# One level of Strassen's product for the mLSTM values and output gates of a hybrid decoder layer

## The reference, cut to what matters

```python
hin = _rms_norm(x, norm_g[0])
z = hin @ w_in                      # (512 x 1024) @ (1024 x 2964)
(mq, mk, mv, lq, lk, lv, lo, li, lf,
 nq, kc, vc, ksl, vsl, kwn, vwn, ng) = jnp.split(z, split_points, axis=-1)
...
qk = silu(causal_conv(concat([lq, lk])))     # 4 groups of 128 features
y_ml = mlstm(lq, lk, lv, li + gate_b[0], lf + gate_b[1])
y = concat([head_norm(y_moba), head_norm(y_ml) * sigmoid(lo), head_norm(y_nsa)])
```

## Time and profile before

| | before |
|---|---|
| median of 3 runs | 603.61 us |
| the profiled execution | 603.88 us |
| its span | 602.1 us |
| PE busy | 590.5 us (98%) |
| DVE, ACT, POOL busy | 390.1, 300.0, 257.0 us |

### The profile page before, as it was taken

One profiled execution on the slowest core, in us unless ns is written; L12 is line 12 of the kernel. 1 busy time (PEld: TensorE's weight loads), 2 busy tenths in 40 slices (PEclk: granted clock), 3 DMA queues, 4 the chain that ended last, 5 costly groups with the idle time before them and its releaser, 6 DMA issues.

```text
span 602.1 us, 8286 instructions
## 1 busy us (share of the span) xinstructions
PE 590.5 (98%) x3095; PEld 484.5 (80%) x3095; DVE 390.1 (65%) x666; ACT 300.0 (50%) x529; POOL 257.0 (43%) x138
## 2 busy tenths in 40 slices
PE   8999999999999999999999999999999999999995
PEld 5898888877866678899878888888888888888884
DVE  6414605266978774983999777585595685771656
ACT  6713414654589934555645545444355265354322
POOL 7763323573094610043357443631723626611611
PEclk9999999999999999999999999999999999999998
DMA  8743282466023710028034340621603404104002
GB/s 326 288 144 137 72 208 71 87 161 208 1 45 104 264 63 0 1 72 280 1 143 137 136 144 1 209 71 67 202 12 139 141 0 153 57 1 175 1 35 106
DMA packets 36580, 67.18 MB, mean 112 GB/s; under 512 B 2876, under 2 KB 23612, under 8 KB 35516
## 3 DMA queue, kind: packets, MB, share of 16 engines
q1 hardware_dynamic: 36236, 66.25, 34.0%
q10 hardware_dynamic: 304, 0.39, 0.3%
HBM read 62.18 MB, written 2.10 MB: 107 GB/s over the span
## 4 chain that ended last, share of the span: by engine, by line
PE 89%; ACT 4%; DVE 3%; issue 2%; DMA 1%; SPq 0%; POOLq 0%; POOL 0%; ACTq 0%; DVEq 0%
PE ps L1814 19%; PE ps L1816 19%; PE ps L1815 19%; PE ps L2288 7%; PE ps L2290 7%; PE ps L2289 7%; PE ps L2140 2%; PE ps L2155 2%; PE ps L2051 1%; PE ps L2052 1%; ACT probs L949 1%; DMA x_land<-in_x_turned 1%; ACT W L890 1%; PE ps L1979 1%; PE ps L2216 1%
## 5 line engine op out<-in xcount | busy, mean ns | idle before, releaser
L1814 PE MATMUL ps<-xT_h,ring_h 128*128 128x512 f32 (+1 forms) x384 | 144.3, 376 | 0.3 <-DVE q_far L1361 0.3
L1816 PE MATMUL ps<-xT_h,ring_l 128*128 128x512 f32 (+1 forms) x384 | 143.2, 373 | 0.0
L1815 PE MATMUL ps<-xT_l,ring_h 128*128 128x512 f32 (+1 forms) x384 | 143.1, 373 | 0.0
L773 POOL TENSOR_TENSOR ring_l<-raw_d,ring_h 128x1024 fp32r<-128x1024 f32 x25 | 67.3, 2699 | 129.8 <-ACT ring_h L1044 129.8
L773 POOL TENSOR_TENSOR ring_l<-raw,ring_h 128x1024 fp32r<-128x1024 f32 x31 | 76.7, 2499 | 77.5 <-DVE xres L1630 38.1
L692 POOL TENSOR_TENSOR ring_l<-raw,ring_h 128x512 fp32r<-128x512 f32 (+2 forms) x26 | 64.2, 2489 | 74.1 <-ACT ring_h L796 74.1
L1724 DVE TENSOR_TENSOR y<-ps,y 128x512 f32<-128x512 f32 x90 | 61.2, 689 | 50.9 <-PE ps L2290 50.6
L1814 PEld LDWEIGHTS ps<-xT_h,ring_h 128*128 128x128 f32 x384 | 72.4, 188 | 14.0 <-issue 1.3
L1816 PEld LDWEIGHTS ps<-xT_h,ring_l 128*128 128x128 f32 x384 | 72.3, 188 | 12.9
L1815 PEld LDWEIGHTS ps<-xT_l,ring_h 128*128 128x128 f32 x384 | 72.4, 189 | 12.5
L2288 PE MATMUL ps<-ring_h,a_h 128*128 128x512 f32 x196 | 76.7, 391 | 0.1
(11 more groups left out here) (276 smaller groups left out, 994.7 us busy)
## 6 DMA issues: line engine op xcount, KB each, us to landing
raw<-in_w_mlp SPq DMA_DIRECT2D x16, 1024.0 KB, 5.6
raw_d<-in_w_mlp SPq DMA_DIRECT2D x16, 1024.0 KB, 6.1
raw<-in_w_groups SPq DMA_DIRECT2D x8, 1024.0 KB, 4.8
xres<-in_x SPq DMA_DIRECT2D x8, 512.0 KB, 6.3
raw<-in_nsa_cmp_w SPq DMA_DIRECT2D x8, 512.0 KB, 6.6
raw<-in_w_groups SPq DMA_DIRECT2D x8, 256.0 KB, 5.5
raw<-in_w_out SPq DMA_DIRECT2D x2, 1024.0 KB, 6.2
raw<-in_w_out SPq DMA_DIRECT2D x4, 512.0 KB, 4.8
```

The costliest lines, as they stand in the source:

```text
L773: nc.gpsimd.tensor_tensor(slot(ring_l, n), slot_source(n), slot(ring_h, n).bitcast(F32), ALU.subtract).then_inc(lo_done, 1)
L1814: nc.tensor.matmul(o, sh, mh, start=start, stop=False)
L1815: nc.tensor.matmul(o, sh, ml, start=False, stop=False)
L1816: return nc.tensor.matmul(o, sl, mh, start=False, stop=stop)
```

## The change

`lv` and `lo` are now one product (512 x 1024 by 1024 x 1024) in Strassen's form (Winograd's variant): seven products of 256 x 512 by 512 x 512, each 24 matmuls of 512 columns. They need four sums of blocks of x (`s_h`, `s_l`), four sums of weight blocks (`t_sum`, made on DVE from landed chunks), and DVE adds of the results. Group B is now the first group, in slabs of 404 columns; then `lq`, `lk`, then the seven products, three of loaded weights and x sums first. Seven chunks (11, 22, T2, 21, T3, T4, T1) have their low halves cut into four POOL instructions of 512 columns.

```diff
-READER = "vvvv" "vvvv" "vvvv" "aaaa" "v" ...
+READER = "vvvv" "vvvv" "vvvvvvvv" "v" ...
+C_11, C_22, C_T2, C_21, C_T3, C_T4, C_T1 = range(C_S, C_S + 7)
+CHUNK_ORDER = [C_LK, C_T1, C_11, C_22, C_21, C_KVS, C_NQ, C_CMP + 2, ...]
 # SP
+                if c == C_22:
+                    sp.wait_ge(xl_ready, NC + 2)
...
 # POOL
+                step = SEQ if C_S <= c < C_KVS or c >= C_WO else n
+            low_half(C_LQ)
+            def sum_low(n, order):
+                pool.wait_ge(xh_ready, NC + order)
+                nc.gpsimd.tensor_tensor(s_l[n][:], s_raw[n][:], s_h[n][:].bitcast(F32), ALU.subtract).then_inc(xl_ready, 1)
+            sum_low(2, 2)
+            sum_low(0, 3)
+            low_half(C_LK)
+            low_half(C_11)
+            sum_low(3, 4)
+            low_half(C_22)
...
-            for c in range(2, C_CMP):
+            for c in range(C_T2, C_MK + 1):
                 low_half(c)
 # ACT
-            high_half(2)
-            for t in range(NT):
-                x_root(t)
-            for c in (3, 4, 5, 6):
-                high_half(c)
+            high_half(C_LQ)
+            x_root(0)
+            x_root(1)
+            act.wait_ge(x_scaled, NC + 3)
+            for n in (1, 2, 0):
+                sum_high(n)
+            x_root(2)
+            x_root(3)
+            high_half(C_LK)
+            sum_high(3)
+            high_half(C_11)
...
+                if n == 2:
+                    high_half(C_T2)
+            for t in range(2):
+                act.wait_ge(part_used, 2)
+                nc.scalar.activation(first_p[t][:], ps[:, t, :], ACT.Copy).then_inc(first_copied, 1)
+            high_half(C_21)
...
+            high_half(C_T3)
+            high_half(C_T4)
+            high_half(C_T1)
+            high_half(C_KVS)
+            high_half(C_NQ)
 # DVE, beside and behind the eight slabs of x
+                if k < 4:
+                    nc.vector.scalar_tensor_tensor(s_raw[2][:, k, :], x_all[:, k, TH:SEQ], gain_cols[:, k:k + 1], ps[:, 4 + k, 0:TH], ALU.mult, ALU.subtract)
+            for k in range(4):
+                last = nc.vector.scalar_tensor_tensor(s_raw[0][:, k, :], ..., ps[:, 4 + k, TH:SEQ], ALU.mult, ALU.add)
+            nc.vector.tensor_tensor(late, late, s_raw[2][:], ALU.add).then_inc(x_scaled, 1)
+            for k in range(4, NC):
+                last = nc.vector.scalar_tensor_tensor(s_raw[3][:, k - 4, :], ..., ps[:, k, TH:SEQ], ALU.mult, ALU.subtract)
+            nc.vector.tensor_tensor(s_l[1][:], late, s_h[1][:].bitcast(F32), ALU.subtract).then_inc(x_scaled, 1)
...
+            def weight_sum(c):
+                if c == C_T3:
+                    made = nc.vector.tensor_tensor(t_sum[0][:], raw[2][:], raw[3][:], ALU.subtract)
+                elif c == C_T2:
+                    made = nc.vector.tensor_tensor(t_sum[1][:], raw[0][:], t_sum[0][:], ALU.subtract)
+                elif c == C_T4:
+                    dve.wait_ge(lo_done, split_no(C_21) + 1)
+                    made = nc.vector.tensor_tensor(raw[1][:], raw[1][:], t_sum[1][:], ALU.subtract)
+                else:
+                    made = nc.vector.tensor_tensor(raw[2][:], raw[2][:], raw[0][:], ALU.subtract)
...
 # PE
-            pe.wait_ge(xl_ready, 2 * NT)
-            token_group(J_B, C_B, BN)
...
             feature_group(J_CONV, C_LQ)
             feature_group(J_CONV + 2, C_LK)
-            token_group(J_LO, C_LO, 512)
+            values_and_gates()
+                product(C_11, *low, 0, 0, True, part_used, ...)
+                product(C_22, s_h[3], s_l[3], 0, 4, True, part_used, ...)
+                product(C_T2, s_h[1], s_l[1], 0, 2, True, part_used, ...)
+                product(C_21, *high, 0, 0, False, job_done, ...)
+                product(C_T3, s_h[2], s_l[2], 0, 2, False, job_done, ...)
+                product(C_T4, *high, TH, 6, True, job_done, ...)
+                product(C_T1, s_h[0], s_l[0], 0, 4, True, job_done, ...)
```

More of the change, by code:

```diff
@@ L170, in group_columns, with loaded @@
     return 0, NC, [({C_LQ: LQ, C_LK: LK, C_NQ: NQ, C_MQ: MQ, C_MK: MK}[c], 256)]
+def loaded(c):
+    return c <= C_MK and c not in SUMMED
 def group_size(c):
@@ L178, in group_at @@
 def group_at(c):
-    return sum(group_size(k) for k in range(c))
-X_PIECE = [SEQ + NC] + [SEQ] * (NC - 1)
+    return sum(group_size(k) for k in range(c) if loaded(k))
+X_PIECE = [NC + SEQ] + [SEQ] * (NC - 1)
 def build(nc, x, norm_g, gate_b, cmp_w1, cmp_w2, w_out, w1, w2, x_turned, w_groups, col_params, pe_turned, out):
@@ L591, in moba_copies @@
                                      mq_lo[half_rows(m), p, :].bitcast(F32)).then_inc(mq_in[p], 16)
-            for c in CHUNK_ORDER[3:]:
+            for c in CHUNK_ORDER:
                 if c == C_WO + 3:
@@ L1843, in first_group @@
                 pe.wait_ge(xf_ready, 1)
-                pe.wait_ge(lv_in[0], 16)
-                for t in range(EARLY_LV):
-                    last = nc.tensor.matmul(ps[:, (J_LV + t) % 8, :], xf[:, t * P:(t + 1) * P], lv_slab(raw, 0), start=True, stop=False)
+                pe.wait_ge(*slab_loaded(0))
+                for t in range(EARLY_B):
+                    last = nc.tensor.matmul(ps[:, J_B + t, 0:BN], xf[:, t * P:(t + 1) * P], slab(raw, 0), start=True, stop=False)
                 last.then_inc(first_used, 1)
@@ L1852, in first_group @@
                     else:
[L1853 to L1856 removed]
+                        pe.wait_ge(slab_low, low_count(k))
+                    for t in range(0 if k else EARLY_B, NT):
+                        last = mm3(ps[:, J_B + t, 0:BN], xT_h[:, k, t * P:(t + 1) * P], xT_l[:, k, t * P:(t + 1) * P],
+                                   slab(ring_h, k), slab(ring_l, k), k == 0, k == NC - 1)
                         if k == NC - 1:
@@ L1860, in first_group, with product @@
                         last.then_inc(part_used, 1)
-            def token_group(j0, c0, n):
-                for q in range(2):
-                    wh, wl = chunk(c0 + q)
-                    for t in range(NT):
-                        if q == 0:
-                            bank_free(j0 + t)
-                        for k in range(4):
-                            kk = 4 * q + k
-                            last = mm3(ps[:, (j0 + t) % 8, 0:n], xT_h[:, kk, t * P:(t + 1) * P], xT_l[:, kk, t * P:(t + 1) * P],
-                                       wh[:, k, :], wl[:, k, :], kk == 0, kk == NC - 1)
-                        if q == 1:
-                            last.then_inc(job_done, 1)
-                        elif t == NT - 1:
-                            last.then_inc(part_used, 1)
+            def product(c, lh, ll, tok, bank, fresh, ends, ready):
+                wh, wl = chunk(c)
+                for t in range(2):
+                    pe.wait_ge(*ready[t])
+                    for k in range(4):
+                        cols_ = slice(tok + t * P, tok + (t + 1) * P)
+                        last = mm3(ps[:, bank + t, :], lh[:, k, cols_], ll[:, k, cols_], wh[:, k, :], wl[:, k, :], fresh and k == 0, k == 3, not fresh)
+                    if ends is job_done:
+                        last.then_inc(job_done, 1)
+                if ends is part_used:
+                    last.then_inc(part_used, 1)
@@ L1878, in feature_group, with token_row @@
+            def token_row():
+                pe.wait_ge(consts, 2)
+                for t in range(NT):
+                    pe.wait_ge(x_rstd, t + 1)
+                    last = nc.tensor.transpose(ps[:, G_BANK, t * P:(t + 1) * P],
+                                               stat[:, R_X + t:R_X + t + 1].to_broadcast([P, P]), ident[:])
+                last.then_inc(row_done, 1)
             def feature_group(j0, c):
```

282 lines of the change are left out of this document (177 added, 105 removed).

## The result

The changed kernel takes 606.37 us (median of 6 runs, 605.47 to 607.12), the kernel before 603.62 (6 runs, 603.07 to 603.81): ratio 1.0046, 95% interval 1.0035 to 1.0056. It is slower by 0.46%. The forecast was 602.6 us, the range 599.5 to 605.3: the time lies outside, and in the span of rival B.

A forecast was written before the change was run, and what follows sets the result against it. PE bounds the kernel, with POOL's low halves close behind. 5.2 us spared, less waits of 1.1 and 3.7, with 0.4 taken back, gain 1.0: 602.9 from 603.88, median 602.6 us, range 599.5 to 605.3.

The forecast's parts named there:

- rival B: PE's 3.7 us stand before T3 lowers the granted clock, slowing matmuls behind it: 604.4 to 608 us; chance 0.14.
- the sum of 602.9: The profiled execution's 603.88 us less a net gain of 1.0 us, everything behind the products moving with PE.
- a wait of 3.7 us: PE waits for POOL's low half of T3, ready at 72.8 us where PE needs it at 69.1.
- the 0.4 us taken back: Added back to the gain: next chunk's first piece begins early, and a silu costs POOL only where a piece is queued.
- PE's saving: Fewer matmuls up to the seventh product's end spare PE 4.9 us, at most 5.4; 5.2 carried.
- The exclusion of POOL and DVE: A DVE instruction with two SBUF inputs locks POOL out: 2.05 us per 2048-column sum, 0.5 per 512-column silu.
- POOL's queue: Low halves from LK at 29.0 us without gaps; PE waits 1.1 us at T2 and 3.7 at T3.
- PE's first phase: Slabs, then LQ at 24.0 us without a wait, LK at 35.4, the seven products from 46.2 us.
- Gain of 1.0 before any clock: 5.2 us saved, less waits of 1.1 and 3.7, plus 0.4 and rounding; ends 0 and 5.2.
- A2: Rival: no collisions, DVE's sums fall in gaps of POOL or its instructions start early: 598.4 to 601.4 us; chance 0.24.
- C: Rival: DVE's differences take 0.75 us each, PE waits 1 to 2 us at LQ: 605.2 to 606 us; chance 0.12.
- The gates: Behind the products, four ACT gates of 0.6 us and no rounding: 0.2 us later, covered by 0.37 us at MQ.

The follow-up runs named there:

- experiment 4: Changed kernel with all four DVE weight sums (T3, T2, T4, T1) taking one operand from PSUM, giving other values: 599.10 us, 0.9929 of the kernel before.
- 7: Changed kernel with each of the seven groups' low halves as one POOL instruction of 2048 columns instead of four of 512: 611.60 us, ratio 1.0127 to before.
- 3: Changed kernel with only T4's and T1's sums on DVE taking one operand from PSUM, giving other values: 600.23 us, 0.9943 of the kernel before.
- 1: Changed kernel with 14 unused matmuls of 512 columns filling PE's wait ahead of T3's product: 603.68 us, ratio 1.0004 to the kernel before.
- 8: Changed kernel with `sel` early, ACT's high half of 21 ahead of the copies, and 21's low half on DVE: 599.99 us, 0.9942 of before.
- 10: Changed kernel with `sel` early, 21's high half ahead of ACT's copies, 21's low half on DVE, T1's sum held until T3's low half is done: 599.62 us, 0.9931.
- 2: Changed kernel with 7 unused matmuls, not 14, ahead of PE's wait for T3's low half: 603.89 us, ratio 1.0010 to the kernel before.
- 5: Changed kernel with the three POOL instructions that fill `sel` moved ahead of LQ's low half: 604.57 us, ratio 1.0014 to the kernel before.
- 9: Changed kernel with only group 21's low half moved from POOL to DVE: 600.46 us, 0.9946 of the kernel before.
- 11: Kernel before, with POOL making the second output-gate chunk's low half four and a quarter times more, so PE waits 4.6 us: 611.04 us, ratio 1.0124.

## Why the prediction was wrong

The step that failed is the clock, a term that the sum of 602.9 puts at nothing behind a wait of 3.7 us, for no other reason than the one against rival B: "3.7 us is not far above 2.9, and one fall says little of how surely the next comes". The wait was forecast (3.7 us, it was 3.4), the fall of the clock behind it was named and priced (+1.8 for 8 matmuls, +5.4 for a product; it was 2.9 for 14, as a matmul cost 0.2 us more, not 0.2268), and yet the kernel was forecast as if the clock stayed. The one row on it showed the clock lower 2.9 us after the last matmul; here it fell at about 72.7 us, 2.5 us after the last one ended (69.79 + 0.39), and it fell after every one of the seven waits of 3.0 us or more in the profiled executions of this study. The forecast should have carried its own wait through: with it, 602.9 + 2.9 = 605.8 us; the profiled execution took 606.76, and LK's late start (0.7 us) and the 0.4 us taken back, both below, account for what is left. That the wait came out so near was partly luck: PE reached the products at 46.99 instead of 46.2 and T3's low half ended 0.7 us late, and the two cancel.

Point by point:
- **PE's saving**: right. 4.9 to 5.2 us was forecast; experiment 4 ends the products at 84.32, 5.3 us sooner than before.
- **The exclusion of POOL and DVE**: right, in kind (7) and size (3, 4). The rule that the prediction cites from the Trainium skill (SBUF — State Buffer, section "SBUF: two separate sides") held: 6.66 us in 7 is 4.6 and 2.05. One step of the working was off: (11.47 - 9.56) / 2 is 0.96 us, not 0.98; the 2.05 us carried on came out all the same.
- **POOL's queue**: right to 0.8 us. LK began at 29.70, not 29.0, since LQ's load landed 1.04 us after ACT was ready for it; T2's wait was 0.8 us (1.1 forecast), T3's low half ended at 73.5 (72.8). The x sums were ready at 21.8 (21.5), with 0.41 us per 256 columns in a row (0.40).
- **PE's first phase**: 0.8 us late at the products, as it had waited 1.9 us for x slabs (0.9 before). This wait differs between executions of one order (0.2 us in 1). It cost nothing here, as PE waits for POOL later on anyway.
- **Gain of 1.0 before any clock**: too high. Without the clock the products would end at 89.9, 0.2 us later than before; with LK's 0.7 us taken off, at 89.2, where the queue written out gave 89.1. The 0.4 us that I took back on top were not there.
- **A2**: out, none of the four sums fell in a gap, though experiments 8 to 10 make the case it describes. **C**: out in its cause; PE doesn't wait at LQ, and the differences took the short duration.
- **The gates**: no new wait stands behind the products in the trace; 3.15 us at the transposes became 2.9 at the end of the span.

Left open: what decides whether the clock falls after waits of 1.8 us (not in the profiled execution of 2, probably in 4 of its 11 runs) up to 3.4 us (in every profiled execution, but not in each run of 5), and why it lasted 14 matmuls in the changed kernel and 8 in the six other cases. Neither was tried further.

## What to carry to other kernels

- Where TensorE at full clock gets a new wait of some 3 us, count the wait and what the clock may take behind it, here 2.9 us on top of 3.4, and 1.6 to 1.7 in the six other cases. The wait of 0.8 us before T2 was followed by no fall. If the wait can't be taken away, matmuls into a bank that is overwritten anyway may keep the clock, as 14 of them did in 1.
- A cut in matmuls moves the bound to whoever prepares their operands. Count that engine's queue with its exclusions first, and give a piece to an engine that has room for it: one low half on DVE (3.36 us there, 5.49 on POOL) turned 0.46% slower into 0.54% faster (9), and with three more moves into 0.69% (10).

## What the runs showed of the hardware that I had not expected

- The granted clock may fall during the wait (at 72.7 us in the changed kernel, 0.8 us before T3's first matmul) or only once the matmuls run again: in 11 it read 1.00 through 4.6 us of idling and 0.52 from 84 us on, 0.6 us behind the restart at 83.45.
- 256 columns of PSUM read eight times over cost DVE no more than 2048 of SBUF (2.28 us each), and left POOL alone: 5.06 us for its four pieces, against 4.99.
